# Two activation halves in one product: gate and up matmuls of 512 columns in a two-block transformer kernel

## Chip, cores and metric

One core of a Trainium2 chip runs the whole computation in one launch. The metric is the device time of that core in microseconds, the median of several runs. The engines are TensorE (PE, with its weight loads as PEld), VectorE (DVE), ScalarE (ACT), GpSimd (POOL) and SyncE (SP), which issues the weight DMAs.

## The reference, cut to what matters

The sequence has 256 positions of 1024 channels in float32. Four SwiGLU feed-forwards alternate with three mixers (attention, a gated recurrence with stick-breaking attention, a state-space branch with block attention). Each feed-forward is

```python
def _rmsnorm(x, g):
    xf = x.astype(jnp.float32)
    r = lax.rsqrt(jnp.mean(xf * xf, axis=-1, keepdims=True) + EPS)
    return (xf * r * g.astype(jnp.float32)).astype(x.dtype)

def _swiglu(x, w_gate, w_up, w_down):
    return (jax.nn.silu(x @ w_gate) * (x @ w_up)) @ w_down
...
    x = x + swiglu(rms_norm(x, ffn_norm[layer]), ffn_w_gate[layer], ffn_w_up[layer], ffn_w_down[layer])
```

with w_gate and w_up of 1024 x 2816 and w_down of 2816 x 1024.

## The kernel before

Every float32 operand of a large product is split into a high part, rounded to the float32r format, and a low part, the rest. A product is the sum of three: high weights with high activations, high weights with low activations, low weights with high activations (`PASSES`). All three accumulate in PSUM.

A feed-forward goes through 22 chunks of the 2816 hidden columns, called items here, `FCH = 22`; four feed-forwards, numbered `ffn` 0 to 3, make 88 items. The activations lie transposed in `hT`, as [128 channels, 8 chunks k, 256 positions], in a high and a low part. `gate_up` computes for one item the gate (`w = 0`) and the up projection (`w = 1`): for each of the 8 chunks k the three products of 128x128 weights with 256 columns, 48 products in all. Gate results of even and odd items (`h`) lie in PSUM banks 4 and 5, up results in 6 and 7; only the first half of a bank, 256 of 512 float32 columns, is used. `down` multiplies an item's activation with its 128 x 1024 slice of w_down: 12 products of 512 columns into banks 0 to 3.

TensorE's order is: gate_up of items 0 and 1, `down` of item 0, then in turn gate_up of item i + 1 and `down` of item i. In the second half of item 1's gate_up stand four small products that broadcast 1/rms over the partitions (`broadcast_rinv`, L450), since the norm's row factor is applied behind the projection.

In each item VectorE scales the gate by the row factor `rB` out of PSUM (L1239), ScalarE applies the silu (L849), VectorE scales the up result (L1244), multiplies (L1248, `prod_done`), and makes act_high and act_low (L1253, L1255, `act_ready`, for which `down` waits). Behind that it makes the low parts of the weights two items ahead (gu_low, L1260) and of the next w_down slice (dn_low, L1264); ScalarE makes their high parts (gu_high L857, dn_high L865), gu_high when the item's products no longer need the buffer (`up_ready`). All weight buffers are double. In the first item of a feed-forward VectorE first copies the broadcast factor to `rB` (`row_scale`, L1202). In the first item of ffn 1 to 3 ScalarE's silu stands behind its gu_high (`late`). Each engine works its instructions in the order of the program; semaphores order the engines against each other.

GpSimd prepares tables for the later mixers beside ffn 1 and ffn 2. ScalarE does some activations for them between items of ffn 1 (`side`).

Of the kernel before, what the change touches and what calls it, by code (L numbers as in the profile page):

```python
# [28 lines left out]
F32R = mybir.dt.float32r  # L29
ACT = mybir.ActivationFunctionType  # L30
ALU = mybir.AluOpType
AX = mybir.AxisListType

P = 128
SEQ = 256
TT = SEQ // P
D = 1024
KC = D // P
# [76 lines left out]
def build(nc, a):  # L115
    with ExitStack() as ctx:
        def sb(name, shape, dtype=F32):
            return ctx.enter_context(nc.sbuf_tensor(name, shape, dtype))
# [4 lines left out]

        x = sb("x", [P, TT, D])

        hT = [sb("hT_" + part, [P, KC, SEQ], F32R) for part in ("high", "low")]
        gu_raw = sb("gu_raw", [P, 2, GU])
        dn_raw = sb("dn_raw", [P, 2, D])
        gu = [sb("gu_" + part, [P, 2, GU], F32R) for part in ("high", "low")]
# [3 lines left out]
        sil_s, prod_s = ffn_s[:, 0:2, :], ffn_s[:, 2:4, :]  # L133
# [15 lines left out]
        def bank(i, n=1):  # L149
            return ps[:, i * 512:(i + n) * 512]  # L150
# [24 lines left out]
        rB = scratch[:, TABLES - 2304:TABLES - 2048]  # L175
# [83 lines left out]
        def in_time(v):  # L259
# [6 lines left out]
            "biasM_loaded", "gu_loaded0", "gu_loaded1", "dn_loaded0", "dn_loaded1", "gpost_loaded", "gpost_ffn2", "gpost_final", "out_stored",  # L266
            "ident_loaded", "first_loaded", "first_high", "first_low",
            "sq_done", "std_ready", "rinv_ready", "rB_psum", "rB_ready", "hT_psum", "hT_high", "hT_low",
            "gate_scaled", "up_scaled", "gelu_done", "vfree",
            "gu_high", "gu_split", "dn_high", "dn_split",  # L270
            "gate_ready", "up_ready", "silu_ready", "prod_done", "act_high", "act_ready", "down_done",
            "ffn_tt0", "mix_tt0",
# [27 lines left out]
        PASSES = ((0, 0), (0, 1), (1, 0))  # L300
# [130 lines left out]
        def _(pe):  # L431
# [27 lines left out]
            def gate_up(h, sl, item, G, first=None, between=None):  # L459

                if first == 0:
                    pe.wait_ge(s["first_low"], 1)
                else:
                    pe.wait_ge(s["gu_split"], item + 1)
                if not isinstance(G, int) or G >= 2:
                    pe.wait_ge(s["prod_done"], G - 1)
                for w in range(2):
                    if first == 0 and w == 1:
                        pe.wait_ge(s["gu_split"], item + 1)
                    for k in range(KC):  # L470
                        if first is not None and w == 0:
                            wait_hT(first, k)
                            if k == 0:
                                wait_hT(first, 1)
                        if between is not None and (w, k) == (1, 0):
                            between()
                        o = (w * KC + k) * P
                        for pw_, px in PASSES:
                            i = nc.tensor.matmul(bank(4 + 2 * w + h)[:, 0:SEQ],  # L479
                                                 gu[pw_][:, sl, o:o + P], hT[px][:, k, :],  # L480
                                                 start=(pw_, px, k) == (0, 0, 0),
                                                 stop=(pw_, px, k) == (1, 0, KC - 1))
                    i.then_inc(s["gate_ready" if w == 0 else "up_ready"], 1)

            def down(h, G, start=False, stop=False):
# [275 lines left out]
        def _(act):  # L761
# [74 lines left out]
            def ffn(f, side={}):  # L836
                base, G0 = FFN_ITEM[f], FCH * f

                def step_of(i, r=None):


                    plain, arrived = during(i, r)
                    h, static = i % 2, r is None
                    sl = (base + i) % 2
                    late = static and i == 0 and f > 0

                    def silu():
                        act.wait_ge(s["gate_scaled"], plain(G0 + 1))
                        nc.scalar.activation(sil_s[:, h, :], sil_s[:, h, :], ACT.Silu) \  # L849
                          .then_inc(s["silu_ready"], 1)  # L850

                    if not late:
                        silu()
                    if not static or base + i + 2 < N_ITEMS:
                        act.wait_ge(gu_loaded[sl], arrived(base + 2))
                        act.wait_ge(s["up_ready"], plain(G0 + 1))
                        nc.scalar.activation(gu[0][:, sl, :], gu_raw[:, sl, :], ACT.Copy) \  # L857
                          .then_inc(s["gu_high"], 1)
                    if late:
                        silu()  # L860
                    if not static or i < FCH - 1:
                        act.wait_ge(dn_loaded[1 - h], arrived(G0 + 1))
                        if not static or G0 + i > 0:
                            act.wait_ge(s["down_done"], plain(G0))
                        nc.scalar.activation(dn[0][:, 1 - h, :], dn_raw[:, 1 - h, :], ACT.Copy) \  # L865
                          .then_inc(s["dn_high"], 1)
# [297 lines left out]
        def _(dve):  # L1164
# [63 lines left out]
            def ffn(f, side={}):  # L1228
                base, G0 = FFN_ITEM[f], FCH * f

                def step_of(i, r=None):
# [4 lines left out]
                    dve.wait_ge(s["gate_ready"], plain(G0 + 1))  # L1236
                    if static and i == 0:
                        row_scale((0, 1, 3, 5)[f], 0)
                    nc.vector.tensor_tensor(sil_s[:, h, :], bank(4 + h)[:, 0:SEQ], rB[:, :], ALU.mult) \  # L1239
                      .then_inc(s["gate_scaled"], 1)  # L1240
                    dve.wait_ge(s["up_ready"], plain(G0 + 1))
                    if not static or G0 + i >= 2:
                        dve.wait_ge(s["act_ready"], plain(G0 - 1))
                    nc.vector.tensor_tensor(prod_s[:, h, :], rB[:, :], bank(6 + h)[:, 0:SEQ], ALU.mult) \  # L1244
                      .then_inc(s["up_scaled"], 1)
                    dve.wait_ge(s["silu_ready"], plain(G0 + 1))
                    dve.wait_ge(s["up_scaled"], plain(G0 + 1))
# [685 lines left out]
```

## Time and profile before

| | |
|---|---|
| median of 3 runs | 1194.6 us (1185.57, 1194.6, 1196.36) |
| the profiled execution's own time | 1188.6 us |
| its span, first to last instruction | 1186.8 us |
| mean granted TensorE clock | 0.976 of full speed |
| PE busy | 1115.5 us, 94% |
| PEld busy | 1033.0 us, 87% |
| DVE busy | 767.1 us, 65% |
| ACT busy | 556.2 us, 47% |
| POOL busy | 209.8 us, 18% |

Times in rows are from the start of the span. L479 stands for the gate and up products, L492 for the down products. Products are pipelined, so the distance between the starts of two is what one costs, not its duration.

### The profile page before, as it was taken

The page shows a single profiled execution, that of the slowest core. Times are in us where ns is not written, and L with a number is a line of the kernel's source. Part 1 is how long each engine was busy: PE and PEld are TensorE (multiplying, and loading weights), DVE is VectorE, ACT ScalarE, POOL GpSimd, SP SyncE. Part 2 cuts the span into 40 slices and gives each one's busy share as a digit, 9 for nine tenths or more (in the row PEclk, how much of TensorE's full clock was granted, in tenths as well). Part 3 has the DMA queues.
Part 4 walks back from the last instruction along what each step waited for, and adds up shares of the span by engine and source line. Part 5 has one row for each costly group of instructions (what it writes and reads, how often), then busy time and mean ns, then how long its engine had stood idle before and what let it go on. Part 6 is the DMA issues. An engine that isn't in the chain of part 4 may idle for free.

```text
span 1186.8 us, 21314 instructions
## 1 busy us (share of the span) xinstructions
PE 1115.5 (94%) x8490; PEld 1033.0 (87%) x8490; DVE 767.1 (65%) x1060; ACT 556.2 (47%) x753; POOL 209.8 (18%) x221
## 2 busy tenths in 40 slices
PE   6999999898999999998986999999999899999997
PEld 6999998896589999997975999999999679999996
DVE  4756566765648877666674598766658347665655
ACT  6534344454647534355645544343442346443433
POOL 0410000131009999000000079200000000000000
PEclk9999999898999999999997999999999989999999
DMA  7654545243035545452441365454533304645440
GB/s 296 249 195 176 194 177 195 89 142 107 1 107 207 204 167 212 169 202 92 174 143 36 123 254 209 174 197 173 199 108 108 144 33 147 235 171 200 172 177 35
DMA packets 34464, 189.63 MB, mean 160 GB/s; under 512 B 3824, under 2 KB 4592, under 8 KB 18032
## 3 DMA queue, kind: packets, MB, share of 16 engines
q1 hardware_dynamic: 31968, 181.42, 42.1%
q10 hardware_dynamic: 2160, 6.50, 1.5%
q0 software_dynamic: 288, 1.05, 0.3%
q8 instruction: 33, 0.54, 0.2%
q14 instruction: 15, 0.12, 0.0%
HBM read 187.90 MB, written 1.05 MB: 159 GB/s over the span
## 4 chain that ended last, share of the span: by engine, by line
PE 84%; DVE 7%; ACT 5%; issue 2%; DMA 1%; POOL 1%; ACTq 0%; DVEq 0%; SPq 0%; POOLq 0%
PE ps L479 42%; PE ps L492 20%; PE ps L529 9%; PE ps L546 5%; DVE gu_low L1175 2%; PE ps L564 2%; PE ps L588 2%; ACT gu_high L795 1%; DMA gu_raw<-in_wgu 1%; PE ps L577 1%; PE ps L750 1%; ACT hT_high L832 1%; PE ps L719 1%; POOL scratch L1681 1%; DVE x L1306 1%
## 5 line engine op out<-in xcount | busy, mean ns | idle before, releaser
L479 PE MATMUL ps<-hT_high,gu_high 128*128 128x256 f32 x1408 | 399.4, 284 | 5.6 <-DVE hT_low L1209 5.6
L479 PE MATMUL ps<-hT_low,gu_high 128*128 128x256 f32 x1408 | 399.1, 283 | 0.0
L479 PE MATMUL ps<-hT_high,gu_low 128*128 128x256 f32 x1408 | 399.0, 283 | 0.0
L479 PEld LDWEIGHTS ps<-hT_high,gu_high 128*128 128x128 f32 x1408 | 270.8, 192 | 9.8 <-issue 3.9
L479 PEld LDWEIGHTS ps<-hT_low,gu_high 128*128 128x128 f32 x1408 | 270.6, 192 | 3.1
L479 PEld LDWEIGHTS ps<-hT_high,gu_low 128*128 128x128 f32 x1408 | 270.6, 192 | 0.0
L857 ACT ACTIVATE gu_high<-gu_raw 128x2048 fp32r<-128x2048 f32 x86 | 164.7, 1916 | 128.7 <-PE ps L479 128.7
L1260 DVE TENSOR_TENSOR gu_low<-gu_raw,gu_high 128x2048 fp32r<-128x2048 f32 x86 | 202.2, 2351 | 15.6 <-ACT gu_high L857 15.5
L1244 DVE TENSOR_TENSOR ffn_s<-scratch,ps 128x256 f32<-128x256 f32 x88 | 36.8, 419 | 167.3 <-PE ps L479 167.3
L1175 DVE TENSOR_TENSOR gu_low<-gu_raw,gu_high 128x2048 fp32r<-128x2048 f32 x40 | 91.6, 2290 | 77.4 <-ACT gu_high L795 77.4
L795 ACT ACTIVATE gu_high<-gu_raw 128x2048 fp32r<-128x2048 f32 x40 | 76.7, 1917 | 134.2 <-PE ps L529 94.6
L849 ACT ACTIVATE ffn_s<-ffn_s 128x256 f32<-128x256 f32 x88 | 36.8, 418 | 215.3 <-DVE ffn_s L1239 215.2
L865 ACT ACTIVATE dn_high<-dn_raw 128x1024 fp32r<-128x1024 f32 x84 | 88.9, 1059 | 60.3 <-PE ps L492 60.3
L492 PE MATMUL ps<-dn_high,act_high 128*128 128x512 f32 x352 | 110.4, 395 | 2.5 <-DVE act_low L1255 2.5
L1264 DVE TENSOR_TENSOR dn_low<-dn_raw,dn_high 128x1024 fp32r<-128x1024 f32 x84 | 110.7, 1317 | 2.2 <-ACT dn_high L865 2.2
L492 PE MATMUL ps<-dn_high,act_low 128*128 128x512 f32 x352 | 109.5, 393 | 0.0
L492 PE MATMUL ps<-dn_low,act_high 128*128 128x512 f32 x352 | 109.5, 392 | 0.0
L492 PEld LDWEIGHTS ps<-dn_low,act_high 128*128 128x128 f32 x352 | 66.4, 189 | 14.8
L492 PEld LDWEIGHTS ps<-dn_high,act_low 128*128 128x128 f32 x352 | 66.5, 189 | 14.5
L492 PEld LDWEIGHTS ps<-dn_high,act_high 128*128 128x128 f32 x352 | 61.0, 190 | 10.8 <-issue 2.9
L529 PE MATMUL ps<-hT_high,gu_high 128*128 128x256 f32 x224 | 64.5, 288 | 5.0 <-DVE gu_low L1175 3.4
L529 PE MATMUL ps<-gu_high,hT_high 128*128 128x256 f32 x208 | 61.1, 294 | 2.6 <-DVE gu_low L1175 2.3
(248 smaller groups left out, 1797.2 us busy)
## 6 DMA issues: line engine op xcount, KB each, us to landing
gu_raw<-in_wgu SPq DMA_DIRECT2D x126, 1024.0 KB, 4.8
dn_raw<-in_wdn SPq DMA_DIRECT2D x88, 512.0 KB, 5.2
x<-in_x SPq DMA_DIRECT2D x2, 512.0 KB, 5.0
gu_raw<-in_wgu SPq DMA_DIRECT2D x2, 512.0 KB, 6.7
scratch<-in_glu ACTq DMA_DIRECT2D x1, 1024.0 KB, 9.7
chw<-in_biasM ACTq DMA_DIRECT2D x1, 1024.0 KB, 8.3
out_x<-scratch SPq DMA_DIRECT2D x4, 256.0 KB, 2.2
s5in<-in_s5in ACTq DMA_DIRECT2D x1, 768.0 KB, 7.0
```

The lines of the kernel that those rows point to most:

```text
L479: i = nc.tensor.matmul(bank(4 + 2 * w + h)[:, 0:SEQ], gu[pw_][:, sl, o:o + P], hT[px][:, k, :], start=(pw_, px, k) == (0, 0, 0), stop=(pw_ ...
L492: i = nc.tensor.matmul(bank(2 * t + half), act_s[px][:, h, t * P:(t + 1) * P], dn[pw_][:, h, half * 512:half * 512 + 512], start=start and ...
L529: i = nc.tensor.matmul(out[:, h * SEQ:(h + 1) * SEQ], lhsT, rhs, start=(pw_, px, k) == (0, 0, 0), stop=(pw_, px, k) == (1, 0, KC - 1))
L546: i = nc.tensor.matmul(out, hT[px][:, k, t * P:(t + 1) * P], gu[pw_][:, item % 2, k * SEQ:(k + 1) * SEQ], start=(pw_, px, k) == (0, 0, 0), ...
L795: nc.scalar.activation(gu[0][:, g % 2, :], gu_raw[:, g % 2, :], ACT.Copy) \
L849: nc.scalar.activation(sil_s[:, h, :], sil_s[:, h, :], ACT.Silu) \
L857: nc.scalar.activation(gu[0][:, sl, :], gu_raw[:, sl, :], ACT.Copy) \
L865: nc.scalar.activation(dn[0][:, 1 - h, :], dn_raw[:, 1 - h, :], ACT.Copy) \
L1175: nc.vector.tensor_tensor(gu[1][:, g % 2, :], gu_raw[:, g % 2, :], gu[0][:, g % 2, :], ALU.subtract).then_inc(s["gu_split"], 1)
L1244: nc.vector.tensor_tensor(prod_s[:, h, :], rB[:, :], bank(6 + h)[:, 0:SEQ], ALU.mult) \
L1260: nc.vector.tensor_tensor(gu[1][:, sl, :], gu_raw[:, sl, :], gu[0][:, sl, :], ALU.subtract).then_inc(s["gu_split"], 1)
L1264: nc.vector.tensor_tensor(dn[1][:, 1 - h, :], dn_raw[:, 1 - h, :], dn[0][:, 1 - h, :], ALU.subtract) \
```

## The change

The high and low activations of a chunk lie side by side in one tile `hT_both`, and the old names are views of it. One product of the high weights takes both, 512 columns, and fills the whole bank: high x high in the first half, high x low in the second. The product of the low weights with the high activations accumulates on the first half. So an item's gate_up has 16 products of 512 and 16 of 256 columns in place of 48 of 256. Outside TensorE, ScalarE copies the second half into the SBUF tile (`gate_rest`, `up_rest`), VectorE adds the first half to it (`gate_sum`, `up_sum`), and the scaling by rB is done in place in SBUF. ScalarE's two copies stand ahead of the silu and between silu and gu_high. The two copies wait for what the first writer of the tile waited for.

```diff
-        hT = [sb("hT_" + part, [P, KC, SEQ], F32R) for part in ("high", "low")]
+        hT_both = sb("hT", [P, KC, 2, SEQ], F32R)
+        hT = [hT_both[:, :, part, :] for part in range(2)]
...
-                        for pw_, px in PASSES:
-                            i = nc.tensor.matmul(bank(4 + 2 * w + h)[:, 0:SEQ],
-                                                 gu[pw_][:, sl, o:o + P], hT[px][:, k, :],
-                                                 start=(pw_, px, k) == (0, 0, 0),
-                                                 stop=(pw_, px, k) == (1, 0, KC - 1))
+                        out = bank(4 + 2 * w + h)
+                        nc.tensor.matmul(out, gu[0][:, sl, o:o + P],
+                                         hT_both[:, k, :, :].rearrange("p a s -> p (a s)"),
+                                         start=k == 0, stop=False)
+                        i = nc.tensor.matmul(out[:, 0:SEQ], gu[1][:, sl, o:o + P], hT[0][:, k, :],
+                                             start=False, stop=k == KC - 1)
...
+                    act.wait_ge(s["gate_ready"], plain(G0 + 1))
+                    if not static or G0 + i >= 2:
+                        act.wait_ge(s["prod_done"], plain(G0 - 1))
+                    nc.scalar.activation(sil_s[:, h, :], bank(4 + h)[:, SEQ:], ACT.Copy).then_inc(s["gate_rest"], 1)
                     if not late:
                         silu()
+                    act.wait_ge(s["up_ready"], plain(G0 + 1))
+                    if not static or G0 + i >= 2:
+                        act.wait_ge(s["act_ready"], plain(G0 - 1))
+                    nc.scalar.activation(prod_s[:, h, :], bank(6 + h)[:, SEQ:], ACT.Copy).then_inc(s["up_rest"], 1)
                     if not static or base + i + 2 < N_ITEMS:
...
-                    nc.vector.tensor_tensor(sil_s[:, h, :], bank(4 + h)[:, 0:SEQ], rB[:, :], ALU.mult) \
+                    dve.wait_ge(s["gate_rest"], plain(G0 + 1))
+                    nc.vector.tensor_tensor(sil_s[:, h, :], bank(4 + h)[:, 0:SEQ], sil_s[:, h, :], ALU.add) \
+                      .then_inc(s["gate_sum"], 1)
+                    dve.wait_ge(s["gate_sum"], plain(G0 + 1))
+                    nc.vector.tensor_tensor(sil_s[:, h, :], sil_s[:, h, :], rB[:, :], ALU.mult) \
                       .then_inc(s["gate_scaled"], 1)
...
-                    nc.vector.tensor_tensor(prod_s[:, h, :], rB[:, :], bank(6 + h)[:, 0:SEQ], ALU.mult) \
+                    dve.wait_ge(s["up_rest"], plain(G0 + 1))
+                    nc.vector.tensor_tensor(prod_s[:, h, :], bank(6 + h)[:, 0:SEQ], prod_s[:, h, :], ALU.add) \
+                      .then_inc(s["up_sum"], 1)
+                    dve.wait_ge(s["up_sum"], plain(G0 + 1))
+                    nc.vector.tensor_tensor(prod_s[:, h, :], prod_s[:, h, :], rB[:, :], ALU.mult) \
                       .then_inc(s["up_scaled"], 1)
```

## Rows read from the trace of the kernel before

**Rows 1.** The page, part 1: busy us (share of the span) xinstructions.

```profile
PE 1115.5 (94%) x8490; PEld 1033.0 (87%) x8490; DVE 767.1 (65%) x1060; ACT 556.2 (47%) x753; POOL 209.8 (18%) x221
```

**Rows 2.** The page, part 4: the chain that ended last, by line.

```profile
PE ps L479 42%; PE ps L492 20%; PE ps L529 9%; PE ps L546 5%; DVE gu_low L1175 2%; PE ps L564 2%; PE ps L588 2%; ACT gu_high L795 1%; DMA gu_raw<-in_wgu 1%; PE ps L577 1%; PE ps L750 1%; ACT hT_high L832 1%; PE ps L719 1%; POOL scratch L1681 1%; DVE x L1306 1%
```

**Rows 3.** That chain in order of time, ffn 0: start, us, what.

```profile
91.51 5.75 PE ps L479 x48
97.26 2.75 PE ps L492 x12
```

**Rows 4.** Timeline of PE, ffn 0: start, us, what.

```profile
63.10 0.63 PE L492 MATMUL ps<-dn_high,act_high 128*128 128x512 f32 x2
...
65.39 0.62 PE L492 MATMUL ps<-dn_high,act_low 128*128 128x512 f32 x2
65.84 0.28 PE L479 MATMUL ps<-hT_high,gu_high 128*128 128x256 f32 x1
65.96 0.28 PE L479 MATMUL ps<-hT_low,gu_high 128*128 128x256 f32 x1
```

**Rows 5.** Timeline of DVE, late in ffn 1.

```profile
506.18 0.42 DVE L1244 TENSOR_TENSOR ffn_s<-scratch,ps 128x256 f32<-128x256 f32 x1 [2.54 <-PE ps L479]
506.70 0.42 DVE L1248 TENSOR_TENSOR ffn_s<-ffn_s 128x256 f32<-128x256 f32 x1
...
507.49 0.42 DVE L1255 TENSOR_TENSOR act_low<-ffn_s,act_high 128x256 fp32r<-128x256 f32 x1
508.10 2.29 DVE L1260 TENSOR_TENSOR gu_low<-gu_raw,gu_high 128x2048 fp32r<-128x2048 f32 x1 [0.18 <-ACT gu_high L857]
510.31 1.22 DVE L1264 TENSOR_TENSOR dn_low<-dn_raw,dn_high 128x1024 fp32r<-128x1024 f32 x1
```

**Rows 6.** Timelines of ACT, DVE and PE, first items of ffn 0.

```profile
25.62 0.42 ACT L849 ACTIVATE ffn_s<-ffn_s 128x256 f32<-128x256 f32 x1 [2.78 <-DVE ffn_s L1239]
...
26.06 0.42 DVE L1248 TENSOR_TENSOR ffn_s<-ffn_s 128x256 f32<-128x256 f32 x1 [0.85 <-ACT ffn_s L849]
...
27.42 4.58 PE ps L492 x12
```

**Rows 7.** Windows, first items of ffn 0, with granted clock (PEclk).

```profile
28.40:31.90 3.50, 3.50 (x10) 2.70 (x9) 3.50 (x4) 0.62 (x2) 0.00 (x0) 0.51 1.03 394
```

**Rows 8.** Timeline of DVE and the chain, first items of ffn 1.

```profile
366.88 0.42 DVE L1202 COPY scratch<-ps 128x256 f32<-128x256 f32 x1 [1.22 <-PE ps L450]
...
369.11 0.57 DVE L1255 TENSOR_TENSOR act_low<-ffn_s,act_high 128x256 fp32r<-128x256 f32 x1
...
369.83 2.96 PE ps L492 x12
```

**Rows 9.** Timeline of DVE, one round in ffn 2 beside GpSimd.

```profile
697.07 0.41 DVE L1239 TENSOR_TENSOR ffn_s<-ps,scratch 128x256 f32<-128x256 f32 x1
697.40 0.40 DVE L1244 TENSOR_TENSOR ffn_s<-scratch,ps 128x256 f32<-128x256 f32 x1
697.96 0.76 DVE L1248 TENSOR_TENSOR ffn_s<-ffn_s 128x256 f32<-128x256 f32 x1 [0.16 <-ACT ffn_s L849]
...
699.39 0.80 DVE L1255 TENSOR_TENSOR act_low<-ffn_s,act_high 128x256 fp32r<-128x256 f32 x1
...
704.42 0.41 DVE L1239 TENSOR_TENSOR ffn_s<-ps,scratch 128x256 f32<-128x256 f32 x1
```

**Rows 10.** Groups of instructions, DVE, 690 to 760 us: busy, mean ns.

```profile
L1239 DVE TENSOR_TENSOR ffn_s<-ps,scratch 128x256 f32<-128x256 f32 x9 | 3.7, 411 | 0.0
L1248 DVE TENSOR_TENSOR ffn_s<-ffn_s 128x256 f32<-128x256 f32 x9 | 5.2, 574 | 1.0 <-ACT ffn_s L849 0.3
```

**Rows 11.** Windows: PE, PEld, DVE, ACT, POOL busy; clock; DMA.

```profile
380.00:465.00 85.00, 85.00 (x601) 80.09 (x600) 69.04 (x73) 40.73 (x43) 81.49 (x62) 1.00 0.54 197
690.00:750.00 60.00, 60.00 (x425) 56.48 (x424) 52.15 (x56) 25.57 (x23) 55.98 (x56) 1.00 0.58 209
```

More of the change, by code:

```diff
@@ L268, in build @@
             "sq_done", "std_ready", "rinv_ready", "rB_psum", "rB_ready", "hT_psum", "hT_high", "hT_low",
-            "gate_scaled", "up_scaled", "gelu_done", "vfree",
+            "gate_scaled", "up_scaled", "gate_sum", "up_sum", "gate_rest", "up_rest", "gelu_done", "vfree",
             "gu_high", "gu_split", "dn_high", "dn_split",
```

## The prediction

> **What bounds the kernel now.** I read the page first: TensorE is busy for 94% of the span [rows 1], and the chain that ended last lies for 42% of the span on the gate and up products (L479) and for 20% on the down products (L492) [rows 2]. Then the same chain in order of time: in the feed-forwards it is nothing but 48 gate and up products in 5.75 us and 12 down products in 2.75 us, an item of 8.50 us, again and again (one stands for all, [rows 3]). No other engine stands in it after the first item. So a product saved there is time saved, as long as the rest keeps pace.
>
> The prices follow from it. 5.75 / 48 is 0.12 us for a product of 256 columns, and two of them start that far apart (65.84 to 65.96). 2.75 / 12 is 0.229 us for one of 512, as in the 12 of them that start at 63.10 and end where the next item starts, at 65.84 [rows 4]. Twice 0.12 is 0.24: a product carries about 0.012 us that doesn't grow with its columns.
>
> **TensorE's part.** For each of 16 (w, k) the change makes three narrow products into a wide and a narrow one. 48 x 0.12 = 5.76 becomes 16 x (0.229 + 0.12) = 5.58, 0.18 us less for each item, and 88 items make 15.8 us. The trace has no wide product between narrow ones, but it has the transition: the last pair of wide ones (65.39) takes 0.45 until the first narrow one starts (65.84), and the next narrow one follows at the usual 0.12 [rows 4]. It costs nothing of its own. Bounds: if a wide product among narrow ones cost its two halves, 0.24, the gain is 0; if the narrow one behind a wide one cost only half of that, 0.1145, it is 15.8 + 1408 x 0.0055 = 23.5 us. I take 15.8, the value of the pairs. An item is then 8.32 us.
>
> A rule speaks against even this. The Trainium skill (TensorE: Matmul & The Clock Gate, Back-to-back issue gap) has a gap of columns over the clock plus 2.5 ns, of which the change could save 2.5 ns x 1408, an estimate of 3.5 us. Here the gap is 120 ns for 256 columns [rows 4], more than that rule gives, so the row decides; by the rule alone the sum below would be about 12 us worse.
>
> **What is added.** For each item ScalarE copies two 128x256 halves out of PSUM and VectorE adds each to the other half; the scaling by rB, once read from PSUM, becomes a third pass over SBUF. The nearest ScalarE row of that shape is the silu, 0.42 us [rows 6], the VectorE row from PSUM 0.42 as well [rows 5]. That is 0.84 us more on either engine. In the steady state there is room: VectorE's cycle has an idle stretch ahead of the up scaling (2.54 us). Between dependent instructions lie 0.04 us, and 0.10 ahead of the product (506.18 + 0.42 to 506.70). What counts is the latency, at four places.
>
> *End of each feed-forward.* From up_ready to the end of act_low are 1.73 us now (506.18 to 507.49 + 0.42) [rows 5]. A copy (0.46) and a sum (0.46) make it 2.65; with 0.13 ahead and 0.14 behind, 2.92 against 2.75 of down products of the item before, which cover it. About 0.15 us sticks out, four times: 0.6.
>
> *First items of ffn 1 to 3.* VectorE waits for the broadcast of 1/rms and then works in a row: the rB copy at 366.88, act_low until 369.68, the down products at 369.83 [rows 8]. Gate scaling to product is 0.91 us of it now; with sum 0.46, scaling (an instruction that needn't wait for it starts 0.33 later, 697.07 to 697.40 [rows 9]; I take 0.35), sum 0.46 and scaling 0.52 it is 1.79. So TensorE stalls 0.88 longer, and the 0.09 saved in the last half of the second item is hidden too. Each ffn: 22 x 0.18 - 0.97 = 3.0 us gained; three make 9.0.
>
> *First items of ffn 0.* ScalarE issues DMAs until 25.6, and only then do the silu (25.62) and the product (26.06) follow; TensorE's 12 down products wait until 27.42 [rows 6]. ScalarE is in order, so the first copy now stands where the silu stood: copy 0.46, sum 0.46, scaling 0.46, silu 0.34 until the next can start, copy 0.46, sum 0.46, scaling 0.52 put the product 3.16 behind 25.62, 2.7 later than now. The two first items' gain is hidden by it: 20 x 0.18 - 2.7 = 0.9 us gained. Behind that wait TensorE runs at a granted clock of 0.51, its lower level of 1.2 GHz, from 28.4 to 31.9 [rows 7], so the 12 products last 4.58 [rows 6]. With a longer wait more of the low stretch may fall in idle time, or a second one may follow: -1 to +2, and I take 0.
>
> *Where GpSimd works beside VectorE.* The slack is smallest behind the first items. In the times of ffn 1, act_low of item 0 ends at 369.68 + 0.88 - 0.27 (saved by TensorE ahead of the broadcast) = 370.3. VectorE then has 2.2 us of gu_low, 1.2 of dn_low [rows 5], 3.0 from gate sum to product (below) and up to 1.9 for the product, act_high and act_low of item 1: 378.6. TensorE does its down products from 370.4 and another gate_up, 2.75 + 5.58, and wants item 1 at 378.8: 0.2 us of slack beside GpSimd, 1 us where it is idle. Behind it VectorE works without a pause until it has caught up. Where GpSimd is idle such a round is about 7.3 us (2.2 gu_low and 1.1 dn_low, each 0.1 less than its row, as the next starts a little ahead of its end [rows 5]; 0.9 gate sum and scaling, 0.8 silu and copy behind each other on ScalarE, 1.0 up sum and scaling, 1.2 for the rest) and catches up on 8.32. Beside GpSimd it doesn't. From one gate scaling to the next are 7.35 us now (697.07 to 704.42), gate scaling to product 0.89 of it [rows 9]. That 0.89 becomes 0.46 + 0.61 + 0.34 + 0.46 + 0.46 + 0.67 = 3.0, so a round is 9.45 us, 1.1 longer than TensorE's item: the down products wait for act_low.
>
> In these 3.0 I gave each in-place scaling 0.15 us more than 0.42, since in this stretch the product, which reads two operands in SBUF, takes 0.574 and the scaling out of PSUM 0.411 [rows 10]. The Trainium skill (SBUF — State Buffer, Who interferes with whom) says the same of VectorE instructions with two SBUF inputs against GpSimd instructions that read SBUF; the change moves two instructions of an item from the kind that is spared to the kind that isn't. The trace agrees by the two means just given.
>
> GpSimd is busy for 56.0 of 60 us in ffn 2 (690 to 750) and 81.5 of 85 in ffn 1 (380 to 465) [rows 11], some 6 and 9 rounds. At 1.1 us each that is 6.6 and 9.9. But ffn 1's mixture is milder: VectorE is busy for 69.0 of 85 us there, 81%, against 52.2 of 60, 87% [rows 11], which makes its rounds some 0.5 us shorter; and its slack is larger at first (about 1 us). I take 4 us for each, bounds 0 (the slack holds) and 23 for both (the rival below).
>
> **The sum.** -0.9 - 9.0 + 0.6 + 8 = -1.3 us against the profiled execution's own 1188.6 (span 1186.8, 1.8 around it): 1187.3. That execution lies 6.0 below the median of the three runs (1194.6) and 3.6 below their mean of 1192.2. I set the forecast at their mean less about 2: 1190. The runs spread over 0.9%, so within 1% is what a measurement here can hardly tell from no change.
>
> **Rivals.**
>
> *VectorE becomes the bound (slower).* From the point where the round beside GpSimd passes 8.32 us, every such item pays. At 9.8 us (both scalings held as long as act_low is at 699.39, 0.80 instead of 0.42 [rows 9], 0.23 more each than in the 9.45) 15 rounds pay 1.5 each, 22.5 less 0.5 of slack, and the sum is -9.3 + 22 = +12.7; on 1191.3, where the forecast's -1.3 gives 1190, that is 1204. For: the slack is 0.3 to 1 us, and TensorE has no spare item. Against: the loads of VectorE are lighter in half of ffn 1's rounds. Chance 0.2.
>
> *The stalls don't come, and narrow products get cheaper (faster).* With GpSimd's stretch absorbed, -9.3: 1182, still within 1%. With the upper bound of TensorE's gain as well, -9.3 - 7.7 = -17: 1174. For it speaks that TensorE can load weights for longer behind a wide product; against it that the first narrow one behind a wide one shows no gain [rows 4]. Chance of over 1% faster 0.17.
>
> *The wide product saves nothing.* If it costs 0.24, TensorE's 15.8 is gone, the first items still cost 2.7 + 3 x 0.9, the ends 0.6, the GpSimd stretch some 6: +12, 1203. Against: 0.229 in every pair. Chance 0.04, and it is counted with the slower ones. The gap rule of the Trainium skill weighed above would come out near this rival, with its estimate of 3.5 us for the whole saving.
>
> **How the numbers follow.** The forecast's case, a small gain on TensorE that first items and GpSimd's stretch eat up, has 0.6; with the ends of the rivals that lie within 1%, same is 0.61, faster 0.17, slower 0.22. The range reaches from near the upper bound of TensorE's gain (1174; 1177, since that end leaves out a tenth) to the rival with VectorE as the bound, taken just short (1203).
>
> **What would show it.** On TensorE: an item of 8.32 us in the chain late in ffn 1 and all through ffn 3, wide products 0.229 after which the narrow one starts, 0.12 to the next. At the start of ffn 0 the down products at about 30.1. In ffn 1 and 2 waits of TensorE (L492's row) on act_low of about 1 us per item while GpSimd runs, none behind it. In-place scalings near 0.57 there and 0.42 elsewhere, sums at 0.42 everywhere. I am wrong if items of ffn 3 aren't shorter by 0.18, if no such waits show, or if they go on behind GpSimd's work.

## The result and the profile after

The changed kernel takes 1205.88 us, median of 4 runs (1205.44 to 1208.83), beside 1191.05 for the kernel before in 4 runs of the same comparison: ratio 1.013, 95% interval 1.0073 to 1.0187. It is slower, by 14.8 us. A second comparison gave 1206.58 beside 1189.4, ratio 1.0147 (1.0095 to 1.0198). The forecast was 1190, with a range up to 1203.

The profiled execution took 1206.04 us, span 1204.2, mean granted clock 0.967; that of before 1188.6, 1186.8 and 0.976. Page of the changed kernel, parts 1 and 4, beside [rows 1, 2]:

```profile
PE 1116.4 (93%) x7082; PEld 962.9 (80%) x7082; DVE 840.4 (70%) x1236; ACT 606.8 (50%) x929; POOL 206.3 (17%) x221
...
PE 71%; DVE 15%; ACT 7%; issue 4%; DMA 1%; ACTq 1%; POOL 1%; DVEq 0%; SPq 0%; POOLq 0%
PE ps L480 21%; PE ps L494 16%; PE ps L483 11%; PE ps L531 9%; PE ps L548 5%; DVE gu_low L1278 3%; DVE dn_low L1282 2%; PE ps L590 2%; PE ps L566 2%; DVE gu_low L1185 2%; ACT gu_high L797 1%; DVE ffn_s L1266 1%; DMA gu_raw<-in_wgu 1%; PE ps L579 1%; DVE ffn_s L1262 1%
```

L480 is the wide product, L483 the narrow one, L494 the down products. TensorE has 1408 instructions fewer, VectorE 176 more and ScalarE 176 more (two for each of 88 items). What to see is the chain: VectorE has 15% of it, and its lines are those of the feed-forward, in-place scaling, product, gu_low and dn_low (L1262, L1266, L1278, L1282). In [rows 2] none of its lines for an item is named. TensorE waits for VectorE now.

The chain in order of time in ffn 3 and the timeline of PE there, beside [rows 3, 4]:

```profile
1122.80 0.24 PE ps L480
1123.04 0.12 PE ps L483
...
1123.39 0.12 PE ps L483
```

```profile
1122.99 0.40 PE L480 MATMUL ps<-hT,gu_high 128*128 128x512 f32 x1
1123.23 0.28 PE L483 MATMUL ps<-hT,gu_low 128*128 128x256 f32 x1
1123.34 0.63 PE L494 MATMUL ps<-dn_high,act_high 128*128 128x512 f32 x2
...
1126.09 0.39 PE L480 MATMUL ps<-hT,gu_high 128*128 128x512 f32 x1
```

By the mean of the starts in ffn 3 a pair is 0.353 us from wide start to wide start, 16 of them 5.65, the down products 2.74: an item is 8.39 us, 0.11 less than before. The forecast had 8.32. The narrow product is 0.117, a little under 0.12, but the wide one is 0.236, not 0.229.

Where the time came from is best read from the starts of the down-product groups (L492 before, L494 after) of the two timelines of PE: the first and the last of 21 in each feed-forward. This table is worked out from them:

| at | before, us | after, us | after less before |
|---|---|---|---|
| ffn 0, first | 27.42 | 30.19 | +2.8 |
| ffn 0, last | 199.10 | 199.53 | +0.4 |
| ffn 1, first | 369.83 | 375.69 | +5.9 |
| ffn 1, last | 539.89 | 551.21 | +11.3 |
| ffn 2, first | 687.48 | 701.01 | +13.5 |
| ffn 2, last | 857.55 | 875.52 | +18.0 |
| ffn 3, first | 1003.51 | 1022.62 | +19.1 |
| ffn 3, last | 1173.59 | 1190.44 | +16.9 |
| end of span | 1186.8 | 1204.2 | +17.4 |

Inside ffn 0 and 3 the change gains 2.3 us each. Inside ffn 1 and 2 it loses 5.5 and 4.4: their 20 distances are 175.52 and 174.51 us long, where 20 x 8.39 is 167.8. That excess, 7.7 and 6.7, is GpSimd's stretch. In ffn 1 the distances begin 8.87, 11.79, 11.05, in ffn 2 8.70, 9.66, 9.67, 9.67, 9.66, 9.68; then both fall to 8.4 to 8.8 and end at 8.39.

One such round of 9.66 us in ffn 2, timeline of DVE of the changed kernel (it answers to [rows 9]):

```profile
742.67 0.41 DVE L1250 TENSOR_TENSOR ffn_s<-ps,ffn_s 128x256 f32<-128x256 f32 x1
743.11 0.51 DVE L1253 TENSOR_TENSOR ffn_s<-ffn_s,scratch 128x256 f32<-128x256 f32 x1
744.45 0.42 DVE L1259 TENSOR_TENSOR ffn_s<-ps,ffn_s 128x256 f32<-128x256 f32 x1 [0.83 <-ACT ffn_s L863]
744.91 0.99 DVE L1262 TENSOR_TENSOR ffn_s<-ffn_s,scratch 128x256 f32<-128x256 f32 x1
746.00 0.66 DVE L1266 TENSOR_TENSOR ffn_s<-ffn_s 128x256 f32<-128x256 f32 x1
...
750.77 1.63 DVE L1282 TENSOR_TENSOR dn_low<-dn_raw,dn_high 128x1024 fp32r<-128x1024 f32 x1
752.33 0.41 DVE L1250 TENSOR_TENSOR ffn_s<-ps,ffn_s 128x256 f32<-128x256 f32 x1
```

The gate sum of the next item (752.33) follows dn_low at once, so VectorE has no slack: this round is its own. The only idle time in it is 0.83 us ahead of the up sum, ended by ScalarE's copy (L863). From the gate sum to the product are 3.33 us where the forecast had 3.0; the rest of the round, 6.33, is what it had (6.45). The miss of 0.33 is the second in-place scaling, 0.99 where 0.57 was counted, less 0.09 that the other steps are shorter. And this is what TensorE sees of it:

```profile
758.05 0.70 PE L494 MATMUL ps<-dn_high,act_high 128*128 128x512 f32 x2 [1.03 <-DVE act_low L1273]
```

The long rounds of ffn 1 have another look, timelines of DVE and of POOL of the changed kernel:

```profile
386.53 3.44 DVE L1282 TENSOR_TENSOR dn_low<-dn_raw,dn_high 128x1024 fp32r<-128x1024 f32 x1
...
393.75 2.45 DVE L1273 TENSOR_TENSOR act_low<-ffn_s,act_high 128x256 fp32r<-128x256 f32 x1
```

```profile
386.50 2.39 POOL L1644 TENSOR_TENSOR scratch<-scratch,chw 128x1024 f32<-128x1024 f32 x1
388.98 4.49 POOL L1648 TENSOR_SCALAR chw<-scratch 128x1024 f32<-128x1024 f32 x1
393.56 2.36 POOL L1644 TENSOR_TENSOR scratch<-scratch,chw 128x1024 f32<-128x1024 f32 x1
```

A tile of 128x256 that takes 0.42 us in [rows 5] takes 2.45 us here, from 393.75 to 396.20, and beside it lies one GpSimd operation of 1024 columns (393.56 to 395.92). dn_low, 1.22 in [rows 5], takes 3.44, beside another of them (386.50). The kernel before had such a hold too, where it cost nothing, since act_low was long done (timeline of DVE, ffn 1, before):

```profile
393.64 3.42 DVE L1264 TENSOR_TENSOR dn_low<-dn_raw,dn_high 128x1024 fp32r<-128x1024 f32 x1
```

In the changed kernel TensorE waits for 3.16 us, and the stretch that begins in this wait runs at its lower level of 1.2 GHz (timeline of PE, and windows with the columns of [rows 11]):

```profile
396.35 1.19 PE L494 MATMUL ps<-dn_high,act_high 128*128 128x512 f32 x2 [3.16 <-DVE act_low L1273]
```

```profile
395.30:402.10 6.80, 5.75 (x14) 4.53 (x15) 5.94 (x6) 6.55 (x15) 3.98 (x5) 0.50 0.22 61
```

The wait makes the distance before it long (11.79), the low clock the one after it (11.05).

### The profile page after: what moved, and what is told of

It is laid out like the page before. It is cut to its first block, busy times and chain, and to the rows that moved or that the text cites. A ratio compares the mean times of both kernels' runs of the same rounds, so it can differ in the third digit from the quotient of the medians.

```text
span 1204.2 us, 19175 instructions
## 1 busy us (share of the span) xinstructions
PE 1116.4 (93%) x7082; PEld 962.9 (80%) x7082; DVE 840.4 (70%) x1236; ACT 606.8 (50%) x929; POOL 206.3 (17%) x221
## 4 chain that ended last, share of the span: by engine, by line
PE 71%; DVE 15%; ACT 7%; issue 4%; DMA 1%; ACTq 1%; POOL 1%; DVEq 0%; SPq 0%; POOLq 0%
PE ps L480 21%; PE ps L494 16%; PE ps L483 11%; PE ps L531 9%; PE ps L548 5%; DVE gu_low L1278 3%; DVE dn_low L1282 2%; PE ps L590 2%; PE ps L566 2%; DVE gu_low L1185 2%; ACT gu_high L797 1%; DVE ffn_s L1266 1%; DMA gu_raw<-in_wgu 1%; PE ps L579 1%; DVE ffn_s L1262 1%
## 5 line engine op out<-in xcount | busy, mean ns | idle before, releaser
L480 PE MATMUL ps<-hT,gu_high 128*128 128x512 f32 x1408 | 503.8, 400 | 5.2 <-DVE hT L1219 5.2
L483 PE MATMUL ps<-hT,gu_low 128*128 128x256 f32 x1408 | 396.4, 281 | 0.0
L480 PEld LDWEIGHTS ps<-hT,gu_high 128*128 128x128 f32 x1408 | 266.3, 189 | 71.0 <-issue 3.7
L483 PEld LDWEIGHTS ps<-hT,gu_low 128*128 128x128 f32 x1408 | 267.5, 190 | 3.1
L1278 DVE TENSOR_TENSOR gu_low<-gu_raw,gu_high 128x2048 fp32r<-128x2048 f32 x86 | 201.2, 2339 | 0.0
L494 PE MATMUL ps<-dn_high,act_high 128*128 128x512 f32 x352 | 112.8, 402 | 17.8 <-DVE act_low L1273 17.5
L1259 DVE TENSOR_TENSOR ffn_s<-ps,ffn_s 128x256 f32<-128x256 f32 x88 | 37.3, 424 | 127.1 <-ACT ffn_s L863 127.1
L1282 DVE TENSOR_TENSOR dn_low<-dn_raw,dn_high 128x1024 fp32r<-128x1024 f32 x84 | 110.1, 1311 | 1.2 <-ACT dn_high L875 1.2
L494 PE MATMUL ps<-dn_low,act_high 128*128 128x512 f32 x352 | 110.4, 395 | 0.0
L494 PE MATMUL ps<-dn_high,act_low 128*128 128x512 f32 x352 | 110.0, 394 | 0.0
L531 PE MATMUL ps<-hT,gu_high 128*128 128x256 f32 x448 | 84.3, 290 | 5.0 <-DVE gu_low L1185 3.4
L494 PEld LDWEIGHTS ps<-dn_high,act_high 128*128 128x128 f32 x352 | 60.6, 191 | 34.5 <-issue 23.9
L857 ACT ACTIVATE ffn_s<-ps 128x256 f32<-128x256 f32 x88 | 33.3, 379 | 96.4 <-PE ps L483 93.8
L531 PE MATMUL ps<-gu_high,hT 128*128 128x256 f32 x416 | 79.1, 292 | 2.2 <-DVE gu_low L1185 1.9
L494 PEld LDWEIGHTS ps<-dn_low,act_high 128*128 128x128 f32 x352 | 67.0, 190 | 15.2
L494 PEld LDWEIGHTS ps<-dn_high,act_low 128*128 128x128 f32 x352 | 66.9, 190 | 14.8
L531 PEld LDWEIGHTS ps<-hT,gu_high 128*128 128x128 f32 x448 | 71.6, 197 | 5.9 <-DVE gu_low L1185 3.6
```

What stands on the lines that cost most here:

```text
L480: nc.tensor.matmul(out, gu[0][:, sl, o:o + P], hT_both[:, k, :, :].rearrange("p a s -> p (a s)"), start=k == 0, stop=False)
L483: i = nc.tensor.matmul(out[:, 0:SEQ], gu[1][:, sl, o:o + P], hT[0][:, k, :], start=False, stop=k == KC - 1)
L494: i = nc.tensor.matmul(bank(2 * t + half), act_s[px][:, h, t * P:(t + 1) * P], dn[pw_][:, h, half * 512:half * 512 + 512], start=start and ...
L531: i = nc.tensor.matmul(out[:, h * SEQ:(h + 1) * SEQ], lhsT, rhs, start=(pw_, px, k) == (0, 0, 0), stop=(pw_, px, k) == (1, 0, KC - 1))
L1259: nc.vector.tensor_tensor(prod_s[:, h, :], bank(6 + h)[:, 0:SEQ], prod_s[:, h, :], ALU.add) \
L1278: nc.vector.tensor_tensor(gu[1][:, sl, :], gu_raw[:, sl, :], gu[0][:, sl, :], ALU.subtract).then_inc(s["gu_split"], 1)
```

## The experiments

My theory after the result had three parts: the wide product costs 0.236 where it alternates; VectorE sets the period beside GpSimd; and it does so because ScalarE's second copy stands behind the silu in an engine that works in order. The rival was that the loss is TensorE's own (other products, more low clock).

Ratios are those to the kernel before, run on the same chip in between.

| kernel | us | before, us | ratio | 95% interval |
|---|---|---|---|---|
| TensorE's part alone | 1183.66 | 1192.79 | 0.9938 | 0.9909 to 0.9968 |
| outside work alone | 1208.34 | 1192.79 | 1.0143 | 1.0106 to 1.0181 |
| products grouped | 1201.99 | 1192.79 | 1.0075 | 1.0047 to 1.0102 |
| copies first | 1194.65 | 1192.79 | 1.0022 | 1.0001 to 1.0043 |
| the change again | 1206.58 | 1189.4 | 1.0147 | 1.0095 to 1.0198 |
| no GpSimd in ffn 2 | 1201.14 | 1189.4 | 1.010 | 1.0062 to 1.0139 |
| grouped, copies first | 1186.37 | 1189.4 | 0.9973 | 0.9944 to 1.0003 |
| the same, DMAs later | 1187.12 | 1189.4 | 0.9971 | 0.9943 to 0.9999 |
| no angle reduction in ffn 1 | 1201.98 | 1193.3 | 1.0098 | 1.0067 to 1.0129 |
| grouped, copies first, again | 1192.25 | 1193.3 | 0.9995 | 0.9963 to 1.0028 |
| the same, side work later | 1188.01 | 1193.3 | 0.9979 | 0.995 to 1.0007 |

### The two halves of the change

**TensorE's part alone.** Products as changed; ScalarE and VectorE as before. The second half of each bank isn't read, so high weights with low activations are left out of the output.

```diff
-                    nc.scalar.activation(sil_s[:, h, :], bank(4 + h)[:, SEQ:], ACT.Copy).then_inc(s["gate_rest"], 1)
...
-                    nc.vector.tensor_tensor(sil_s[:, h, :], bank(4 + h)[:, 0:SEQ], sil_s[:, h, :], ALU.add) \
-                      .then_inc(s["gate_sum"], 1)
-                    nc.vector.tensor_tensor(sil_s[:, h, :], sil_s[:, h, :], rB[:, :], ALU.mult) \
+                    nc.vector.tensor_tensor(sil_s[:, h, :], bank(4 + h)[:, 0:SEQ], rB[:, :], ALU.mult) \
```

> TensorE's part alone: the wide product as in the change, but nothing outside TensorE, so the products of high weights with low activations are computed and left out of the gate and up results. If TensorE's gain is what the profile after shows in undisturbed items (8.39 against 8.50 us), 88 items give 88 x 0.115 = 10 us: 1181 on 1191, ratio 0.992. If the wide product really costs 0.229 once ScalarE and VectorE don't read the other banks beside it, items are 8.32 us and it is 16 us: 1175, ratio 0.987. No wait of the down products on act_low in either case.

Measured: ratio 0.9938, 9.1 us less in the medians. Its distances are 8.39 behind the first of each feed-forward, ffn 1 and 2 last 167.83 and 167.82 us between first and last group, where before's last 170.06 and 170.07. So TensorE's gain is 2.25 / 20 = 0.113 us an item, 88 of them 9.9, and nothing eats it as long as the outside work is as before.

**Outside work alone.** The change, but with three narrow products per chunk, each into its half.

```diff
-                        nc.tensor.matmul(out, gu[0][:, sl, o:o + P],
-                                         hT_both[:, k, :, :].rearrange("p a s -> p (a s)"),
...
+                        for pw_, px in PASSES:
+                            i = nc.tensor.matmul(out[:, px * SEQ:(px + 1) * SEQ],
+                                                 gu[pw_][:, sl, o:o + P], hT[px][:, k, :],
...
```

> The outside part alone: three narrow products as before, but high weights with low activations go to the second half of the bank, and copies, sums and in-place scalings are those of the change. If latency outside TensorE is the loss, this keeps it: about 25 us (17 lost in the profile after, 10 gained by TensorE given back, less some 2 since items of 8.50 us leave more room), 1191 + 25 = 1214, ratio 1.02. If the loss came from how the wide product runs, ratio 1.00.

Measured: 1.4% slower (1208, where I had expected 1214), with 8.50 us late in ffn 1 and in ffn 0 and 3. In ffn 1 the distances are 8.58, 11.58, 9.95, 9.12, in ffn 2 8.83, 9.67, 9.66, 9.68, 9.67. That is the changed kernel's period although TensorE's item is 0.11 longer. PE in ffn 2, timeline:

```profile
740.66 0.70 PE L494 MATMUL ps<-dn_high,act_high 128*128 128x512 f32 x2 [0.95 <-DVE act_low L1273]
```

So the period of 9.67 is VectorE's, and the loss is the outside work's. It also tells why the two parts don't multiply: 0.9938 x 1.0143 = 1.008, the change has 1.013 and 1.0147. In a round that VectorE sets, TensorE's 0.11 is worth nothing. From the lengths of ffn 1 and 2 the outside work costs 7.7 + 6.7 us on the new products (changed kernel less TensorE's part alone), 6.3 + 5.2 on the old ones (outside work alone less before), 2.9 more on the new ones. By the ratios the parts make -7.4 + 17.0 = 9.6 us and the change 15.5 to 17.5; of this difference of 6 to 8 us the 2.9 are one part. The other 3 to 5 us lie within what the ratios leave open, 0.3 to 0.6% each, and go with the clock that the runs were granted (see why the prediction was wrong).

### The parts of the loss

**Products grouped.** For each of gate and up first the eight wide products, then the eight narrow ones.

```diff
                         nc.tensor.matmul(out, gu[0][:, sl, o:o + P],
                                          hT_both[:, k, :, :].rearrange("p a s -> p (a s)"),
                                          start=k == 0, stop=False)
+                    for k in range(KC):
+                        o = (w * KC + k) * P
                         i = nc.tensor.matmul(out[:, 0:SEQ], gu[1][:, sl, o:o + P], hT[0][:, k, :],
...
```

> The change with TensorE's order altered: for gate and for up first the 8 wide products, then the 8 narrow ones. If the wide product costs 0.236 instead of 0.229 because it alternates with narrow ones, wide ones in a row cost 0.229 and items fall from 8.39 to 8.32 or less: some 4 to 6 us less than the change, 1201. If it is the operand (activations of 512 columns as the moving one) or the bank, the wide ones stay at 0.236 and the time at 1206.

Measured: distances of 8.305 and a ratio of 1.0075. The chain in order of time, ffn 3:

```profile
1105.09 1.81 PE ps L480 x8
1106.90 0.95 PE ps L485 x8
1107.85 1.84 PE ps L480 x8
1109.69 0.95 PE ps L485 x8
1110.65 2.75 PE ps L496 x12
```

Eight wide products in a row take 1.81 to 1.84, 0.226 to 0.230 each, what they cost among the down products; eight narrow ones take 0.95, 0.119 each. Alternating, a wide one costs 0.236. The forecast's 8.32 is what the grouped order gives: its price was read from wide products among wide ones. In this kernel, too, the last wide product ahead of a narrow one costs 0.227 (mean of the starts in ffn 3): one transition is free, and only the steady alternation costs 0.006 us more a pair. Why it does is open. The grouped kernel's long rounds stay (ffn 2: 8.89, 9.14, 9.67, 9.66, 9.65).

**Copies first.** ScalarE's second copy stands ahead of the silu; nothing else is moved.

```diff
                     nc.scalar.activation(sil_s[:, h, :], bank(4 + h)[:, SEQ:], ACT.Copy).then_inc(s["gate_rest"], 1)
-                    if not late:
-                        silu()
                     act.wait_ge(s["up_ready"], plain(G0 + 1))
                     if not static or G0 + i >= 2:
                         act.wait_ge(s["act_ready"], plain(G0 - 1))
                     nc.scalar.activation(prod_s[:, h, :], bank(6 + h)[:, SEQ:], ACT.Copy).then_inc(s["up_rest"], 1)
+                    if not late:
+                        silu()
```

> The change with ScalarE's order altered: the copy of the up half stands ahead of the silu, so it is there when VectorE comes for it. In the rounds in which VectorE is behind, the 0.8 us of idle time ahead of the up sum go: rounds of 9.67 us in ffn 2 become about 8.9, that is 5 x 0.8 = 4 us, in ffn 1 some 2 to 3 (two long rounds), at the start of ffn 0 0.8. If latency is the loss, 1206 - 7 = 1199, ratio 1.007. If VectorE's sheer work beside GpSimd is it, 1206.

Measured: ratio 1.0022, some 12 us of the loss given back by where one instruction stands, where I had expected 7. Behind the first all distances of ffn 2 are 8.39 (167.78 in all, 6.7 less than with the change), and in ffn 1 four are longer, 9.72, 8.81, 8.54 and 8.44 (169.77 in all, 5.7 less). The first down products of ffn 0 start at 29.10, 1.1 sooner, and in its profile no low stretch of the clock follows (first distance 8.46 instead of 10.01). A round beside GpSimd, timeline of DVE of this kernel:

```profile
706.12 0.41 DVE L1250 TENSOR_TENSOR ffn_s<-ps,ffn_s 128x256 f32<-128x256 f32 x1
...
706.91 0.42 DVE L1259 TENSOR_TENSOR ffn_s<-ps,ffn_s 128x256 f32<-128x256 f32 x1
707.36 0.43 DVE L1262 TENSOR_TENSOR ffn_s<-ffn_s,scratch 128x256 f32<-128x256 f32 x1
707.89 0.78 DVE L1266 TENSOR_TENSOR ffn_s<-ffn_s 128x256 f32<-128x256 f32 x1
...
714.36 0.41 DVE L1250 TENSOR_TENSOR ffn_s<-ps,ffn_s 128x256 f32<-128x256 f32 x1
```

A round is 8.24 us, under 8.39. The up sum has no idle time ahead of it, and the scaling behind it is shorter too, 0.445 in the mean of this stretch. So the 0.83 us was not only lost by itself: with the copy late, the in-place scaling of the up result also came to lie where GpSimd held it. That second half is read from the means alone; no run separates them.

**No GpSimd in ffn 2.** The 48 elementwise operations of GpSimd's readout table beside ffn 2 are left out; 16 fills stand in their place.

```diff
-                        tt(out, c_im[:, js, :] if part else c_re[:, js, :], (re if part else re)[:, js, :], ALU.mult)
-                        tt(work[:, js, :], c_re[:, js, :] if part else c_im[:, js, :], im[:, js, :], ALU.mult)
-                        tt(out, out, work[:, js, :], op)
+                        step.mark(nc.gpsimd.memset(out, 0.0))
+                        step.done(pool)
```

> The change without GpSimd's 48 elementwise operations beside ffn 2 (the readout table of the state-space branch; zeros are written in their place, so that branch's result is left out). If VectorE's rounds of 9.67 us come from GpSimd's accesses, ffn 2 runs at 8.39 us throughout and is 6.5 us shorter: 1200. If the copy behind the silu alone makes them, they stay and so does the 1206.

Its profiled execution was granted 0.84 of the full clock in ffn 0, where its distances are 9.03, so only its rows of ffn 2 are used; in ffn 2 it was granted 0.95, but its distances are those of full clock. Measured there: 167.80 us from the first to the last group, behind the first all distances 8.39, against 174.48 for the changed kernel in the same comparison; that is 6.7, and the medians differ by 5.4. Groups of DVE, 690 to 760 us, mean in ns, first the changed kernel, then this one:

```profile
L1262 DVE TENSOR_TENSOR ffn_s<-ffn_s,scratch 128x256 f32<-128x256 f32 x7 | 5.8, 833 | 0.2
...
L1271 DVE CAST act_high<-ffn_s 128x256 fp32r<-128x256 f32 x7 | 3.9, 553 | 0.2
L1253 DVE TENSOR_TENSOR ffn_s<-ffn_s,scratch 128x256 f32<-128x256 f32 x7 | 3.5, 497 | 0.2
L1259 DVE TENSOR_TENSOR ffn_s<-ps,ffn_s 128x256 f32<-128x256 f32 x7 | 3.0, 423 | 5.0 <-ACT ffn_s L863 5.0
```

```profile
L1262 DVE TENSOR_TENSOR ffn_s<-ffn_s,scratch 128x256 f32<-128x256 f32 x7 | 3.0, 425 | 0.2
...
L1259 DVE TENSOR_TENSOR ffn_s<-ps,ffn_s 128x256 f32<-128x256 f32 x7 | 3.0, 424 | 6.4 <-ACT ffn_s L863 6.4
...
L1271 DVE CAST act_high<-ffn_s 128x256 fp32r<-128x256 f32 x7 | 2.1, 305 | 0.2
```

Without GpSimd the idle time ahead of the up sum is there all the same (6.4 us) and costs nothing. The loss of ffn 2 needs both, the late copy and GpSimd's hold on VectorE: it is gone without either. The sums, which read one operand from PSUM, are alike in both. The instructions with two operands in SBUF are held, and so is the cast to act_high, which has one (0.553 and 0.305).

**No angle reduction in ffn 1.** The same question for ffn 1: one GpSimd helper with operations of 1024 columns is left out (the tables' angles aren't reduced).

```diff
-            reduce_angle(tabS, tabC, chw[:, 4:8, :], (C1, C2))
```

> The change without GpSimd's four operations of 1024 columns each that bring a table of angles into one period (the angles are clipped instead, so the state-space tables are left wrong). They lie beside items 1 to 3 of ffn 1 and hold VectorE up to 2.4 us at a time. If they make ffn 1's two long rounds (11.7 and 9.9 to 11.1 us), the longest wait of the down products there falls from over 3 us to at most 1.5, and ffn 1 is 3 to 4 us shorter: 1203, ratio 1.011. If the ScalarE work between items 2 and 3 makes them, they stay at 1206.

Measured: ratio 1.0098, against 1.0147 for the changed kernel: 0.0049 less, 5.8 us, but the two intervals overlap, and the lengths say more. ffn 1 lasts 171.59 instead of 174.99, its longest distance is 9.61 instead of 11.66. The longest wait, timelines of PE, of this kernel and then of the changed one in its second comparison:

```profile
400.02 0.70 PE L494 MATMUL ps<-dn_high,act_high 128*128 128x512 f32 x2 [0.73 <-DVE act_low L1273]
```

```profile
394.80 1.19 PE L494 MATMUL ps<-dn_high,act_high 128*128 128x512 f32 x2 [3.11 <-DVE act_low L1273]
```

So the wide GpSimd operations make the long round of ffn 1, and 3.4 of its 7 us. That the rest is the same mechanism as in ffn 2 is argued and not shown; that most of it goes when the copy comes first (169.77) speaks for it.

**The change again.** As changed, run beside the kernel without GpSimd in ffn 2.

> The change itself, run beside the others: 1206, ratio 1.013, with 5 rounds of 9.67 us in ffn 2 and two of over 11 us in ffn 1.

Measured: 1206.58, with ffn 1 at 174.99 and ffn 2 at 174.48 us. The two repeat within 0.6 us.

### Can the loss be taken away?

**Grouped, copies first** is both edits above together.

> The change with both orders altered: the up copy ahead of the silu on ScalarE, and 8 wide products before 8 narrow ones on TensorE. The first alone measured 1194.7, the second brings items from 8.39 to 8.31 us, 88 x 0.08 = 7 us: 1188, ratio 0.996. If items that short leave VectorE behind again beside GpSimd (its rounds are 8.2 us there), some of the 7 come back: 1191.

> The kernel with both orders once more, beside the one with the coefficients later: ratio 0.997 as before, 2.3 us above the other.

Measured: ratios 0.9973 and 0.9995; distances 8.305, ffn 2 166.23 us, ffn 1 168.60 and 169.00. Neither interval leaves 1 out, and the same kernel's two medians, 1186.37 and 1192.25, lie 5.9 apart.

**The same, DMAs later**: ScalarE issues the DMAs of `first_constants` inside ffn 0, behind its first item, not ahead of it.

```diff
-            first_constants()
-            ffn(0, {2: first_exps})
+            ffn(0, {2: first_exps}, early=first_constants)
```

> The kernel with both orders, and the seven DMAs that ScalarE issues ahead of the first item's copies put behind that item's steps. The first copy then stands 3.4 us earlier, the down products of item 0 start near 25.5 instead of 29.1 us, and TensorE's wait there (4 us) goes with the low stretch of the clock behind it: 3.5 to 5 us less than with both orders alone, 1184. If the weights or rB aren't there so early, nothing changes: 1188.

Measured: 0.9971, no better than without (its interval just leaves 1 out). The chain in order of time at the start of ffn 0:

```profile
22.92 0.28 ACT ffn_s L859
...
24.09 0.43 DVE scratch L1215
...
27.68 4.32 PE ps L496 x12
```

The down products start at 27.68, 1.4 us sooner than at 29.05, where I had expected 25.5. The copy (22.92) is no longer late, but now VectorE is: its rB copy comes at 24.09, behind a dn_low. A miss, and a case of a stall that gives way to the next one.

**The same, side work later**: ScalarE's activations for GpSimd's coefficients move in ffn 1 from item 2 to item 8.

```diff
-            ffn(1, {2: s5_coefficients, FCH - 4: lambda: trig_tables(0), FCH - 3: lambda: trig_tables(1)})
+            ffn(1, {8: s5_coefficients, FCH - 4: lambda: trig_tables(0), FCH - 3: lambda: trig_tables(1)})
```

> The kernel with both orders, with ScalarE's coefficient activations put behind item 8 of ffn 1 instead of item 2. VectorE has then caught up when they delay its round and when GpSimd's work behind them starts. The rounds of 9.85, 8.81 and 8.54 us in ffn 1 become about 8.31: 2.3 us less than with both orders alone. If GpSimd's angle reduction, which stays where it is, is what delays VectorE, one round above 9 us remains.

Measured: ffn 1 lasts 167.18 us, 1.8 less than in the kernel without this edit; distances of 8.96 and 8.64 are left, where I had expected 8.31; the ratio, 0.9979, doesn't tell it apart from that one or from the kernel before. No version here beats the kernel before clearly by its ratio. By runs of a like granted clock (0.971 or less; the clocks are taken up below) they are 2 to 7 us faster: medians of 1188.3 (3 runs) and 1193.3 (9) with both orders, 1188.4 (6) with the DMAs later and 1189.8 (9) with the side work later, where the kernel before has 1195.4 (27).

## Why the prediction was wrong

The mechanisms were those of the forecast; two terms of its sum had the wrong size, and a third, less clock, wasn't in it. The outcome is that of the rival in which VectorE becomes the bound, given 0.2: it had rounds of 9.8 us (9.9 by its own addends, 9.45 and twice 0.23), and 9.67 came. That its time, 1204, lies so near is in part luck: it counted the gain of TensorE in full, 15.8 where 9.9 came, and 22 for GpSimd's stretch, where 14.4 came.

- *TensorE's part, 15.8 us: mis-sized, 9.9.* The step that failed is "It costs nothing of its own", which took the price of the alternation from one transition [rows 4]. The wide product costs 0.236 between narrow ones; the item is 8.39, not 8.32. The lengths of ffn 1 and 2 in TensorE's part alone and the grouped order (8.305) show it. Worth 5.9 us.
- *GpSimd beside VectorE, 4 + 4 us: mis-sized, 7.7 + 6.7.* The step that failed is "I take 4 us for each": for ffn 2 the rows had given 6.6 and I took 4, though both reasons to take less, milder rounds and a larger slack at first, were ffn 1's. And for ffn 1 the mean load of VectorE (81%) said nothing of the few wide GpSimd operations, which hold a single instruction for two microseconds; the trace before had a dn_low of 3.42 us there, which I hadn't looked for. In-place scalings were put at 0.57 and had means of 0.50 and 0.83. Worth 6.4 us.
- *First items of ffn 0: right.* The down products came at 30.19, forecast 30.1. The chain in order of time goes copy (L857), sum, scaling, silu, second copy (L863), sum, scaling, product, as added up; its two copies and the up sum:

```profile
25.65 0.39 ACT ffn_s L857
...
27.37 0.37 ACT ffn_s L863
...
27.84 0.44 DVE ffn_s L1259
```

- The clock behind it, put at no loss, was right in the first profile: 0.50 from 30.1 to 33.5, where it had been 0.51 from 28.4 to 31.9 [rows 7]. In the second profile of the changed kernel the low stretch lasts from 29.4 to 36.2, and the first distance is 11.16 us, not 10.01; that lies within the forecast's -1 to +2.

```profile
30.10:33.50 3.40, 3.31 (x8) 2.67 (x9) 3.40 (x3) 0.66 (x2) 0.00 (x0) 0.50 0.73 272
```

- *Ends and other first items: nearly right.* From the last group of one feed-forward to the first of the next the forecast's terms make some 0.8 to 0.9 us (0.15 + 0.97, less what TensorE gains there). Measured from ffn 2 to 3: 1.1; from ffn 1 to 2: 2.2.
- *The stretch where GpSimd is idle: right.* No wait from the middle of ffn 1 on, none in ffn 3, as said.

Put right, the sum is -1.3 + 5.9 + 6.4 = +11.0 us, where the medians show 14.8 and 17.2 (intervals 8.7 to 22 and 11 to 24). In the two profiled executions the rest lies between the last group of ffn 0 and the first of ffn 1: 170.73 us before, 176.16 after, 4.5 more than the forecast's terms. There TensorE was granted less clock, 0.90 by the window from 200 to 370 (0.94 before, 0.91 with TensorE's part alone):

```profile
200.00:370.00 170.00, 150.51 (x938) 125.47 (x937) 101.08 (x210) 90.54 (x204) 27.22 (x41) 0.90 0.27 96
```

But that distance goes up and down from one execution to another: 174.54 for TensorE's part alone, 173.50 for the outside work alone, 173.94 for the change again, 184.47, 176.02 and 172.81 for the grouped kernels (alone, with copies first, with side work later). TensorE's part alone is faster than before with a distance 3.8 longer. All twelve other profiles have more than the 170.73 of the one profile of before, so that one may be the short exception.

The granted clocks of all runs say more than one profile each. The eight runs of the changed kernel were granted 0.966 to 0.971 in the mean, with a median of 1206.0 us. The kernel before was granted 0.967 to 0.982 in 79 runs of the later comparisons; the 27 of them at 0.971 or less have a median of 1195.4. So at a like clock the change costs 10.6 us, near the 11.0 of the sum put right, and the rest goes with the lower clock, for which the forecast had no term. (The match is rough, as a low stretch behind a long wait, as in ffn 1, is in the mean clock too.) The two halves add up in the same way: TensorE's part alone at 0.971 or less has a median of 1185.7 (8 runs), 9.7 less than before; the outside work alone at 0.974 to 0.979 has 1208.1 (5 runs), where before has 1188.2 (32 runs), 19.9 more; together 10.2. Whether the change brings the lower clock isn't settled: 8 of 12 runs of TensorE's part alone and 1 of 6 of the outside work alone are at 0.971 or less, which points to the new products, but without the angle reduction it is 2 of 10.

## What to carry to other kernels

An engine that is busy for two thirds of the time can still be the bound in a stretch: work out the length of its round there, and when it comes out within a few per cent of TensorE's, don't shade the result down. In an engine that works in order, a copy that frees or feeds another engine goes ahead of any instruction that waits for that engine's answer; here one such place was worth some 12 us of a loss of 15 to 17. Two versions whose runs spread over 1% are better compared by runs of a like granted clock than by their medians alone. The price of a product depends on its neighbours, so take it from a row with the same neighbours or keep the range open.

## What the runs showed that I had not expected

- A wide product of 512 columns costs 0.236 us when it alternates with narrow ones of 256 (0.117), and 0.226 to 0.230 in a row (the narrow ones then 0.119).
- Beside GpSimd the same in-place scaling of 128x256 had a mean of 0.833 us, and 0.425 when GpSimd's work was gone; a sum that reads one operand from PSUM kept 0.42. The Trainium skill (SBUF — State Buffer, Who interferes with whom) says that an instruction of VectorE with two inputs in SBUF contends with a GpSimd instruction that reads SBUF, and that one with at most one such input, outside the performance modes that use two ports, doesn't. The trace agrees, by these numbers; how much it costs only the rows say. The cast to act_high, with one input in SBUF, went from 0.305 to 0.553 beside GpSimd all the same; whether it runs in such a mode no row shows.
- How long it holds seems to go with the GpSimd instruction beside it, by two cases: act_low of 128x256 took 2.45 us beside one of 2.36 us, and dn_low 3.44 beside one of 2.39, where it takes 1.22 in [rows 5].
